# First expert's tokens picked by one-hot products on PE, instead of fetched by DMA

## The reference

```python
hf = rms_norm(x, g).reshape(-1, D_MODEL)
top_v, top_i = lax.top_k(hf @ w_router, 2)
gates = softmax(top_v)
combine = einsum('tk,tke->te', gates, one_hot(top_i, 8))
for e in range(8):
    he = silu(hf @ w_eg[e]) * (hf @ w_eu[e])          # 3584 wide
    y = y + combine[:, e:e + 1] * (he @ w_ed[e])
```

## Time and profile before

| | |
|---|---|
| median of 3 runs | 1600.28 us (1599.96 to 1600.9) |
| the profiled execution | 1599.89 us, span 1598.1 us |
| mean granted clock of PE | 0.971 of full speed |
| PE busy | 1536.2 us (96% of the span) |
| DVE busy | 1243.9 us (78%) |
| ACT busy | 973.6 us (61%) |
| POOL busy | 87.8 us (5%) |
| read and written in DRAM | 422.55 MB and 9.14 MB |

### The profile page before, as it was taken

One profiled execution on the slowest core, in us unless ns is written; L12 is line 12 of the kernel. 1 busy time (PEld: TensorE's weight loads), 2 busy tenths in 40 slices (PEclk: granted clock), 3 DMA queues, 4 the chain that ended last, 5 costly groups with the idle time before them and its releaser, 6 DMA issues.

```text
span 1598.1 us, 22314 instructions
## 1 busy us (share of the span) xinstructions
PE 1536.2 (96%) x7942; PEld 1293.6 (81%) x7942; DVE 1243.9 (78%) x1293; ACT 973.6 (61%) x1086; POOL 87.8 (5%) x85
## 2 busy tenths in 40 slices
PE   6997999999988979999999999999999999999997
PEld 5986999999965968878887887887887887887886
DVE  6995545447785458888889889889889888889885
ACT  6564443344544247676677777667677667677673
POOL 1001110011320010000000000000000000000000
PEclk9998999999977979999999999999999999999999
DMA  8930344444360149989989998998998998997992
GB/s 340 179 117 27 111 166 162 164 161 159 134 227 21 53 169 356 355 308 396 353 340 379 338 368 354 340 368 347 363 362 330 373 359 320 378 365 310 394 347 106
DMA packets 64323, 431.40 MB, mean 270 GB/s; under 512 B 7861, under 2 KB 10165, under 8 KB 13712
## 3 DMA queue, kind: packets, MB, share of 16 engines
q1 hardware_dynamic: 57312, 412.38, 67.4%
q0 software_dynamic: 3616, 12.28, 3.3%
q10 hardware_dynamic: 3344, 6.05, 1.1%
HBM read 422.55 MB, written 9.14 MB: 270 GB/s over the span
## 4 chain that ended last, share of the span: by engine, by line
PE 89%; DVE 3%; issue 3%; ACT 2%; DMA 1%; POOL 1%; ACTq 0%; DVEq 0%; POOLq 0%
PE bank L332 26%; PE bank L334 26%; PE bank L333 26%; PE bank L370 3%; PE bank L722 1%; PE bank L354 1%; ACT d_hi L1024 1%; DVE oe_lo L1563 1%; PE bank L588 1%; PE bank L700 1%; PE bank L701 1%; PE bank L668 0%; PE bank L674 0%; PE bank L614 0%; PE bank L577 0%
## 5 line engine op out<-in xcount | busy, mean ns | idle before, releaser
L1414 DVE TENSOR_TENSOR w_lo<-land,w_hi 128x2048 fp32r<-128x2048 f32 x224 | 503.9, 2288 | 95.4 <-ACT w_hi L1021 93.8
L1021 ACT CAST w_hi<-land 128x2048 fp32r<-128x2048 f32 x224 | 417.6, 1912 | 3.5 <-issue 3.5
L332 PE MATMUL bank<-w_hi,xe_hi 128*128 128x512 f32 x896 | 366.8, 409 | 0.5 <-DVE xe_lo L1500 0.5
L333 PE MATMUL bank<-w_lo,xe_hi 128*128 128x512 f32 x896 | 354.9, 396 | 0.0
L334 PE MATMUL bank<-w_hi,xe_lo 128*128 128x512 f32 x896 | 354.4, 396 | 0.0
L1024 ACT CAST d_hi<-land 128x2048 fp32r<-128x2048 f32 x112 | 213.9, 1911 | 129.5 <-PE bank L334 129.5
L1511 DVE TENSOR_TENSOR d_lo<-land,d_hi 128x2048 fp32r<-128x2048 f32 x112 | 256.7, 2292 | 25.8 <-ACT d_hi L1024 19.0
L334 PEld LDWEIGHTS bank<-w_hi,xe_lo 128*128 128x128 f32 x896 | 168.6, 188 | 41.0
L332 PEld LDWEIGHTS bank<-w_hi,xe_hi 128*128 128x128 f32 x896 | 168.6, 188 | 34.0 <-DVE xe_lo L1500 0.9
L333 PEld LDWEIGHTS bank<-w_lo,xe_hi 128*128 128x128 f32 x896 | 169.2, 189 | 32.5
L332 PE MATMUL bank<-d_hi,heT_hi 128*128 128x512 f32 x448 | 177.9, 397 | 3.4 <-DVE heT_lo L1542 3.4
(11 more groups left out here) (241 smaller groups left out, 2141.1 us busy)
## 6 DMA issues: line engine op xcount, KB each, us to landing
land<-in_w_expert SPq DMA_DIRECT2D x336, 1024.0 KB, 5.7
land<-in_w_dense SPq DMA_DIRECT2D x54, 1024.0 KB, 4.9
rel_rows<-rb POOLq DMA_DIRECT2D x1, 3072.0 KB, 36.0
bias<-rel_rows ACTq DMA_DIRECT2D x4, 512.0 KB, 4.8
X<-in_x SPq DMA_DIRECT2D x4, 288.0 KB, 5.7
out_y<-X SPq DMA_DIRECT2D x2, 576.0 KB, 4.2
Us<-in_state POOLq DMA_DIRECT2D x1, 1088.0 KB, 9.4
out_conv_s<-Us POOLq DMA_DIRECT2D x1, 1088.0 KB, 8.5
```

Source lines behind the costliest of these rows:

```text
L332: pe.matmul(out, w[0], x[0], start=start, stop=False)
L333: pe.matmul(out, w[0], x[1], start=False, stop=False)
L1021: act.copy(w_hi[n % RING][:], land[(DENSE + u) % LAND][:]).then_inc(hi_done, 1)
L1414: dve.tensor_tensor(w_lo[n % RING][:], land[slot][:], w_hi[n % RING][:].bitcast(F32), ALU.subtract).then_inc(split, 1)
```

## The change

For the first trip the token rows are not fetched. PE multiplies the rows in `H_tok`, as weights, with `pick`, as moving operand (`pick_first`): for each of 8 blocks of 128 columns three products, one for each tile of tokens, with 128, 128 and 32 weight rows. The result lies where the transposes put theirs. `slot_rows` of trip 0 goes behind the picks and to `bank[6]`. POOL's first `gather_rows` is left out, and the counts of `xt_ready` are one lower. ACT casts the second down unit after `xe_split` and waits for the stores of `H_tok` ahead of `silu`, which overwrites it. DVE does the trip count right after `place(0)`, then `xe_rest`, the fourth unit's `expert_lo`, `slot_row_of`, `expert_down_lo(0, 0)`, `gated(0, 0)`, `expert_down_lo(0, 1)`.

```diff
             def gather(trip, h):
-                pe.wait_ge(xt_ready, 16 * (trip + 1))
+                pe.wait_ge(xt_ready, 16 * trip)
...
+            def pick_first(h):
+
+                for k in range(4):
+                    a = (4 * h + k) * P
+                    for i, (t0, nt) in enumerate(TT):
+                        last = pe.matmul(bank[4 + h][:, P * k:P * k + P], H_tok[0:nt, i, a:a + P], pick[0:nt, i, :],
+                                         start=(i == 0), stop=(i == 2))
+                last.then_inc(gathered, 1)
+
+            pe.wait_ge(htok_ready, 6)
+            pe.wait_ge(htok_scaled, 3)
             pe.wait_ge(P_ready, 1)
-            slot_rows(bank[0])
-            pe.wait_ge(htok_ready, 6)
-            gather(0, 0)
-            gather(0, 1)
+            pick_first(0)
+            pick_first(1)
+            slot_rows(bank[6])
             pe.wait_ge(route_ready, 1)
...
@@ ACT
             expert_hi(0, 0, 2)
-            expert_hi(0, 1, 2)
             act.wait_ge(route_ready, 1)
...
             xe_split(0, 0)
             xe_split(0, 1)
+            expert_hi(0, 1, 2)
+            act.wait_ge(h_stored, 48)
             silu(0, 0)
...
@@ DVE
             place(0)
-            slot_row_of(1, bank[0])
-            dve.wait_ge(gate_kept, 1)
-            dve.tensor_copy(slot_gate[:], next_gate[:]).then_inc(gates_ready, 1)
-
...
-            expert_lo(0, *FIRST_UNITS[3])
-            expert_down_lo(0, 0)
             xe_rest(0, 0)
             xe_rest(0, 1)
+            expert_lo(0, *FIRST_UNITS[3])
+            slot_row_of(1, bank[6])
+            dve.wait_ge(gate_kept, 1)
+            dve.tensor_copy(slot_gate[:], next_gate[:]).then_inc(gates_ready, 1)
+            expert_down_lo(0, 0)
+            gated(0, 0)
             expert_down_lo(0, 1)
-            gated(0, 0)
...
@@ POOL
             pool.wait_ge(h_stored, 48)
             pool.wait_ge(zero_stored, 16)
-            gather_rows(0)
             pool.wait_ge(route_ready, 1)
```

## The result

The changed kernel takes 1606.51 us (median of 7 runs, 1605.70 to 1608.36) against 1600.55 us (7 runs, 1599.88 to 1601.93): ratio 1.0037, 95% interval 1.0025 to 1.0049. It is 6.0 us slower; 7.3 were forecast. The profiled execution took 1606.62 us for a span of 1604.8.

A forecast was written before the change was run, and what follows sets the result against it. PE bounds the kernel, busy 96% of 1598.1 us, so delay ahead of the expert loop counts in full. First expert product +6.9 us and clock +0.4 give +7.3 on 1600.28: 1607.6 us, range 1605.5 to 1610.

The forecast's parts named there:

- The wait goes, 9.58 us with all that belongs to it: Router to first expert: slot rows, fetch wait, transposes, half the cast and subtraction leave the path, 9.58 us.
- A record 0.213 us, a run with one row count 0.30 more: PE's picks at half clock: 48 records at 0.213 us plus 0.30 per run of one row count, 15.0 us.
- Case C: Rival for the picks: row-count changes hidden, picks cold at 10.2 us, total +2.5 us; chance 0.07.
- Half clock during the picks: PE's clock before the first expert product: stays at 0.50 for all of the picks, which take 15.0 us.
- case B: Rival for the picks: they bring the clock up, total -0.3 us, or +1.7 if 9 us in; chance 0.15.
- Slot rows 1.5 us, first expert product +6.9 us: PE behind the picks: slot rows take 1.5 us to 587.6, so the first expert product starts 6.9 us later.
- The clock's extra delay, 0.4 us: First expert's products on PE: the clock may come up later after their start than today, adding 0.4 us.
- DVE, ACT, SP and POOL at nothing: Engines besides PE: their reordered or later work is covered and adds nothing to the time.
- Unit 8: SP's queue: this unit waits for d_lo of chunk 0 and issues about 592.6, 13 us later, still covered.
- case D: Rival on SP's queue: its late unit starves PE, some 3 us on top, +10 us; chance 0.03.
- Total +7.3: Whole kernel: first expert product 6.9 us later plus 0.4 us for the clock, forecast 1607.6 us.
- the lower end of the range: The main forecast's own range, 1605.5 to 1610, from change price (0.8 us), clock (0 to 1.6) and slot rows (0.3).

The follow-up runs named there:

- experiment 1: The kernel before, row fetch kept, with only the changed orders on ACT and DVE: 1600.48 us, ratio 0.9999.
- experiment 2: The changed kernel with the third tile zero-padded, so all 24 pick products have 128 weight rows: 1596.02 us, ratio 0.9970 against the kernel before.
- experiment 3: The changed kernel with the same pick products, the 32-row ones grouped behind the 128-row ones in each half: 1599.67 us, ratio 0.9990 against the kernel before.
- experiment 4: The changed kernel without the third product of each pick block, leaving out 32 tokens: 1595.19 us, ratio 0.9969 against the kernel before.
- experiment 6: The changed kernel with 5 + 4 dense products in PE's two idle stretches ahead of the picks: 1605.48 us, ratio 1.0028 against the kernel before.
- the second profiles: The kernel before and the changed kernel, unaltered, each profiled once more: 1600.3 us (one run) and 1606.32 us (6 runs).
- experiment 5: The kernel before with 12 dense products on PE in its wait for the row fetch: 1597.42 us, ratio 0.9984.
- experiment 7: The changed kernel with padded picks and 5 + 4 dense products ahead of them: 1595.44 us, ratio 0.9973 against the kernel before.

## Why the prediction was right

- *The wait goes, 9.58 us with all that belongs to it.* Right: 9.58 and 9.60 us in the two profiles of before, 9.52 in experiment 1, and no wait of PE in its place.
- *A record 0.213 us, a run with one row count 0.30 more.* Right: 15.03 us against 15.0. It was worked out from two rows in attention with another row count (64); the starts of the single records show it (0.35 to 0.38 us at a change, 0.213 elsewhere, as forecast), and experiments 2 and 3 by taking the changes of row count away. Between two records at half clock the price came out exactly; at full clock a change cost 0.19 us in experiment 3, where 0.17 was forecast from one row. Case C (the changes hidden, as weight loads pulled ahead would have it) is refuted by the 15.03 us. In the grouped order, from the start at half clock, the first 19 records took 4.4 us, 0.23 each.
- *Half clock during the picks.* Right in both profiles, 16.4 us long. The forecast rested on a likeness to other busy stretches that had stayed low, and had no cause to give. What experiments 2, 3 and 4 add is that this too came from the alternation: with the short products grouped, padded or left out, the clock came up 3.0 to 5.5 us into the picks in all four profiles. The single times say that it is no certainty either way: most runs of the grouped order were slower and at a lower mean clock than its profile, and one run of experiment 6 was likely at full clock through alternating picks. Whether the clock is held down by the pauses at the changes (0.22 us of the weight loads each, 3.4 in all, and none with padding) or by the share of 32-row records in each stretch wasn't told apart. The rule of the Trainium skill quoted for case B, that activity of PE releases the throttle ("TensorE: Matmul & The Clock Gate", "What's actually happening"), holds in those three experiments and not in the change, if busy time in the profile is taken as activity; the measurement decides.
- *Slot rows 1.5 us, first expert product +6.9 us.* Right, +6.83, and +6.81 between the second profiles (16.41 against 9.60).
- *The clock's extra delay, 0.4 us.* The term of chance: 1.3 us between the first two profiles (6.1 against 3.1 us of delay, 0.45 us each), nothing between the second two (3.4 against 3.5).
- *DVE, ACT, SP and POOL at nothing.* Right by experiment 1 and by the waits in the profile after. Unit 8 was forecast at 592.6 and went out at 592.27. PE's waits behind the start are seven for heT_lo, 2.4 us in all, as before, so case D did not occur.
- *Total +7.3.* 6.0 measured. The term missing is behind the loop, and the forecast doesn't speak of it: 0.5 to 1.6 us less between the last transposes of he and the end of the span (13.6 and 13.9 us against 15.2 and 14.4), part of it in the landing of the last store, 2.8 us against 4.2 and 3.5. With the row fetch in place experiment 1 has 14.1 us there with a landing of 3.0, and experiment 5 has 13.7 with 2.8, so this looks like the execution and not the change; why the kernel before drew the longer landings in both its profiles stays open. In the first pair of profiles the clock's 1.3 us more and these 1.6 us less cancelled, which is luck.
- *Two slips in the working.* It takes the transposes of he to begin at 590.73; they begin at 590.57, so what the half clock costs the expert products is 1.5 us and not 1.7. And the terms given for the lower end of the range come to +5.8 us, 1606.1, not 1605.5. Neither changes the forecast of +7.3 or what was ruled out.

The version that beats both kernels is the change with the third tile padded, 3.7 to 5.1 us below the kernel before by the medians, and with dense products ahead 4.5 to 5.1. Picking by products was not what cost the time; the third tile's 16 records of 32 rows between the others were.

## What to carry to other kernels

Before products replace a transfer on PE, cost them at the clock that PE has at that place, and by records (two for each fp32 product), and count how often the number of weight rows changes between them: each run of one row count costs 0.30 us at half clock over its records. Zero the rows of a short tile and use all 128, or group the short products: the padded kernel was 0.8 us slower by the medians than the one that left the tile out, and padding was the surer of the two, since most runs of the grouped order gained less than its profile. Where PE must wait anyway, dense products into an unused bank can make what follows start at full clock. That was worth some 2 us in the wait of 5.6 us of experiment 5. It is no sure thing: in experiments 6 and 7 the clock had fallen again when the picks began.

## What was not expected of the hardware

- Products that keep PE busy without a gap in the profile can leave the clock at half for as long as they last: 16.4 us of picks and slot rows, in all three profiles that alternate. The same 48 records in another order had it at full speed 4.4 us in, in the one execution that was profiled. PE's own row hid the difference; the row of its weight loads showed it, 12.80 us busy of 16.42 with alternation and 2.90 of 2.90 with padding.
- A product with 32 weight rows between products with 128 cost more than a product with 128 rows: with the third tile 15.03 us, without it 6.15, with it padded 7.00 and 8.21.
- The clock came up before the picks in experiments 6 and 7 and fell again at 568.9, although PE was busy 2.70 and 3.18 us of the 3.30 before. The router's sums were over by then in both (at 568.6 and 567.7); in experiment 6 the four dense products were under way, and in experiment 7 they had just ended (at 568.8).
